# The expert loop of a decoder layer: four turns and seven steps behind it in place of three and twelve

## The chip, the cores and the metric

One core of one Trainium2 chip runs the whole layer. The time is that of one execution on the device, in microseconds (us), the median of several runs. A profile comes from one execution; its span is the time from the first to the last instruction that it recorded, so that the time of a run lies a little above it.

## What is computed

One decoder layer over 256 positions of 1024 features in float32: attention of two kinds and an output projection, then a mixture of experts. Each position takes 4 of 32 experts, and almost the whole traffic is the experts' weights, 8 MB for gate and up and 4 MB for down, per expert. Cut to the part that matters here:

```python
D_MODEL, SEQ, N_EXPERTS, TOP_K, D_FF = 1024, 256, 32, 4, 1024

def clamped_swiglu(h):
    x_glu = jnp.minimum(h[..., :D_FF], SWIGLU_LIMIT)
    x_lin = jnp.clip(h[..., D_FF:], -SWIGLU_LIMIT, SWIGLU_LIMIT)
    return x_glu * jax.nn.sigmoid(SWIGLU_ALPHA * x_glu) * (x_lin + 1.0)

def moe_ffn(h, w_router, b_router, w_gate_up, b_gate_up, w_down, b_down):
    ...
    logits = (xf @ w_router + b_router).astype(jnp.float32)
    top_vals, top_idx = lax.top_k(logits, TOP_K)
    gate = jax.nn.softmax(top_vals, axis=-1)
    ...
    def expert_block(args):
        xb, e = args
        hgu = xb @ w_gate_up[e] + b_gate_up[e]
        return clamped_swiglu(hgu) @ w_down[e] + b_down[e]
    ...
        x = x + moe_ffn(h2, w_router[l], b_router[l], w_gate_up[l], b_gate_up[l], w_down[l], b_down[l])
```

## The kernel before, in words

The front part (to about 165 us of the profile) is attention, the output projection and the router. Behind it stands a chain of steps, one for each expert and block of up to 64 positions; where no expert has more than 64 positions, as in the profiled data, there are 32 steps, 0 to 31.

**A step.** `step(n, it, g)` on TensorE does, in this order: `up` (the product with gate and up weights of expert k, in two pieces j = 0, 1, L1694), `gather` (the rows of a later expert, L1678), `down` (the down product of expert k-1, L1706), and `between` (turning the gathered rows, L1686, the slots, L1713, the up result, L1720, and adding the result of an earlier expert to the sum in four PSUM banks, L1728). ScalarE and VectorE have a `step` of their own each that copies and works on the results between these products. All of them keep step by semaphores.

**The weights.** They come in pieces of 4 MB, three for a step (up 0, up 1, down), into a ring of five pairs of slots (`pairs`, `NPAIR` = 5, the tiles `pair0` to `pair4`). The queue of SyncE (SP) issues the transfers, one whole piece each (`fetch`, L447), each as soon as TensorE has told by `used0` to `used4` that the pair is free (`free`). The last pieces of all are issued in parts (`rows_in_place`, L363), so that TensorE can start on the first rows while the others are on their way. `landed` and `arrived` are the waits of TensorE for a piece.

**The two places outside the ring.** Two buffers of 2 MB, `extra` and `extra2`, are loaded in the front part with the lower half (rows 4 to 7 of 8) of the down weights of two experts. They are read at the steps `KEPT` = (FIRST + 1, FIRST + 2), numbered from the end of the loop, and the ring brings only the upper half of those two. Which experts they are follows from `expert_behind`. Between these two steps TensorE also does what it owes the sum once: `keep_rows` adds the residual (L1647), `gated_bias` the gated biases of down (L1642), after a transpose of the gates (L1873).

**The loop.** Steps 0 to 4 are written out in front (`FIRST` = 5). Then every engine has a hardware loop (`Fori`) with a body of five steps (`NSTEP`), and behind it `LAST` steps written out. `GROUPS` holds the number of turns for one, two, three or four blocks of 64 positions per expert; the first entry, for one block, is ceil((32 - FIRST - LAST) / 5). The count is read from a register, and a second number, `shift`, skips the places that stay empty. The last two of the `LAST` steps have forms of their own, with the split transfers, and a last down product in two halves of the columns (L1946) with its own combine (L1959).

```python
        def expert_behind(n):
            return E - FIRST - LAST + n
...
            for c in range(first, last - 2):
                expert = expert_behind(expert_of(c))
                if c in (piece(n, 2) for n in KEPT):
                    free(c, groups)
                    rows_in_place(c % NPAIR, expert, 2, 0, 2, f"ring{c % NPAIR}")
                else:
                    fetch(c, groups, expert)
```

Of the kernel before, what the change touches and what calls it, by code (L numbers as in the profile page):

```python
# [43 lines left out]
PAIRS = ((4, 5), (0, 1), (6, 7), (2, 3), (8, 9))  # L44
NPAIR = len(PAIRS)
NSTEP = 5
FIRST, LAST = 5, 12
GROUPS = [-(-(E * (r + 1) - FIRST - LAST) // NSTEP) for r in range(ROUNDS)]
NPOS = NSTEP * GROUPS[-1] + FIRST + LAST + 1
SLOTW = 512 * DK  # L50
# [1946 lines left out]
```

How the kernel before makes its waits and increments, by code:

```python
        def front_arrived(eng, i):  # L279
            eng.wait_ge(s[f"stage{i % NSLOT}"], 16 * (i // NSLOT + 1))
# [10 lines left out]
        def landed(eng, c, g=None):  # L291
            n = 16 * (c // NPAIR + 1)
            eng.wait_ge(s[f"ring{c % NPAIR}"], n if g is None else g * (16 * USES) + n)
# [1 line left out]
        def arrived(eng, c, g=None):  # L295
            if c in PARTS:
                eng.wait_ge(s[PARTS[c][0]], 16 * PARTS[c][1])
            landed(eng, c, g)
# [1 line left out]
        def consumed(eng, c, g=None):  # L300
            n = c // NPAIR + 1
            eng.wait_ge(s[f"used{c % NPAIR}"], n if g is None else g * USES + n)
# [23 lines left out]
        def front_used(eng, i):  # L326
            kind, m = LOADS[i]
            if kind == "in":
                eng.wait_ge(s["proj_full"], NT * (m + 1))
            elif kind == "cmp":
                eng.wait_ge(s["h_full"], m + 1)
            else:
                eng.wait_ge(s["wo_full"], m + 3)
# [3 lines left out]
        @block.sync  # L337
# [27 lines left out]
            front_used(sp, 4)  # L365
            rows_in_place(0, 0, 0, 0, 2, "stage4")
            front_used(sp, 5)
            rows_in_place(0, 0, 0, 2, 4, "ring0")
            front_used(sp, 6)
            rows_in_place(1, 0, 1, 0, 2, "stage0")
            sp.wait_ge(s["u_full"], 1)
            rows_in_place(2, 1, 0, 0, 2, "stage6")
            front_used(sp, 7)
            rows_in_place(1, 0, 1, 2, 4, "ring1")
            sp.wait_ge(s["o_full"], 1)
            rows_in_place(2, 1, 0, 2, 4, "ring2")
            sp.wait_ge(s["oc_half"], 3)
            rows_in_place(4, 0, 2, 0, 2, "down0")
```

## Time and profile before

| | us |
|---|---|
| median of 3 runs | 1067.37 |
| lowest, highest | 1065.93, 1068.52 |
| span of the profiled execution | 1064.8 |
| TensorE busy in it | 1018.3 |

In the rows below, a line of the order of time reads: start (us), length (us), engine, line of the code, operation, result and operands by their names, number of instructions merged, and in brackets the idle time of the engine just before, with what ended it. A line of the windows reads: stretch, its length, TensorE's busy time with the number of instructions that started there, the granted clock as a share of full speed, the busy share of the DMA engines, and GB/s. Instructions are pipelined and lines are merged, so that the end of a line can reach a little into the next. `pair`, without its number, stands for each of the five pairs.

### The profile page before, as it was taken

The numbers are of one execution on the slowest core, as the hardware profiler recorded it, in microseconds if no ns is written. First come the engines' busy times: TensorE is split into PE (matmuls) and PEld (weight loads), VectorE is DVE, ScalarE is ACT, GpSimd is POOL, SyncE is SP. The second block draws the span as 40 slices with busy tenths as digits, with TensorE's granted clock in tenths as the row PEclk, the third lists the DMA queues.
The fourth block names the chain that finished last, engine by engine and source line by source line (L and its number), as shares of the span: only waits on it lengthen the run. The fifth ranks groups of instructions, "written<-read, shape, count | busy, mean of one in ns | idle before, by whom it ended". The sixth has DMA issues, their size and how long they took to land.

```text
span 1064.8 us, 12012 instructions
## 1 busy us (share of the span) xinstructions
PE 1018.3 (96%) x4969; PEld 410.9 (39%) x4969; DVE 293.2 (28%) x676; ACT 167.9 (16%) x325; POOL 15.9 (1%) x42
## 2 busy tenths in 40 slices
PE   8999999999999999999999999999999999899998
PEld 5555644333333333333333333333333333333334
DVE  1764614222222222211222122222112222222222
ACT  2434321111111111110110011111101111110011
POOL 4100000000000000000000000000000000000000
PEclk9999998999999999999999999999999999999999
DMA  9992668999999999999999999999999999999996
GB/s 295 363 409 84 251 263 320 426 424 435 431 430 430 432 429 431 431 433 432 432 431 430 432 432 433 433 432 429 429 429 429 431 433 431 431 432 431 420 425 264
DMA packets 36023, 426.45 MB, mean 400 GB/s; under 512 B 3782, under 2 KB 12062, under 8 KB 19728
## 3 DMA queue, kind: packets, MB, share of 16 engines
q1 hardware_dynamic: 34224, 424.78, 94.9%
q0 software_dynamic: 704, 1.04, 0.5%
q8 instruction: 29, 0.48, 0.2%
q10 hardware_dynamic: 1056, 0.07, 0.1%
q14 instruction: 10, 0.08, 0.0%
HBM read 424.83 MB, written 1.05 MB: 400 GB/s over the span
## 4 chain that ended last, share of the span: by engine, by line
PE 62%; DMA 34%; DVE 2%; SPq 1%; issue 1%; ACT 0%; ACTq 0%; DVEq 0%
DMA pair<-in_w_down 30%; PE bank L1694 24%; PE bank L1706 14%; PE bank L1316 5%; DMA pair<-in_w_gate_up 4%; PE bank L1728 4%; PE bank L1591 3%; PE bank L1678 2%; PE bank L1720 2%; PE bank L1686 1%; PE bank L1713 1%; PE bank L1388 1%; PE bank L1946 1%; SPq L363 1%; PE bank L1348 1%; DMA stage<-in_w_in 1%
## 5 line engine op out<-in xcount | busy, mean ns | idle before, releaser
L1694 PE MATMUL bank<-pair,xs 128*64 128x512 f32 x2048 | 450.0, 594 | 21.9 <-DMA pair<-in_w_gate_up 20.8
L1694 PEld LDWEIGHTS bank<-pair,xs 128*64 128x64 f32 x2048 | 143.1, 137 | 323.3 <-issue 285.9
L1706 PE MATMUL bank<-pair,sig 128*64 128x512 f32 x960 | 212.2, 593 | 13.4 <-DMA pair<-in_w_down 13.4
L1209 DVE COPY gu<-bank 128x512 f32<-128x512 f32 x32 | 36.5, 1140 | 416.2 <-PE bank L1694 416.2
L1706 PEld LDWEIGHTS bank<-pair,sig 128*64 128x64 f32 x960 | 72.3, 137 | 149.2 <-issue 143.4
L757 ACT COPY gu<-bank 128x512 f32<-128x512 f32 x32 | 36.4, 1138 | 457.1 <-PE bank L1694 457.1
L854 DVE TENSOR_TENSOR xs<-bank,gt 128x512 f32<-128x512 f32 x31 | 21.4, 691 | 220.6 <-PE bank L1686 220.6
L1316 PE MATMUL bank<-stage,xt 128*128 128x512 f32 x160 | 72.2, 598 | 0.0
L1728 PE MATMUL bank<-ys,pgt 64*128 64x512 f32 x248 | 61.6, 615 | 0.3 <-ACT ys L762 0.3
L1678 PE MATMUL bank<-xr,onehot 128*64 128x512 f32 x248 | 58.5, 592 | 0.0
L762 ACT COPY ys<-bank 128x512 f32<-128x512 f32 x31 | 18.1, 585 | 206.2 <-PE bank L1706 206.2
L1216 DVE TENSOR_TENSOR gu<-bank,bias_t 128x512 f32<-128x512 f32 x64 | 41.0, 682 | 2.7 <-PE bank L1720 2.7
L1316 PEld LDWEIGHTS bank<-stage,xt 128*128 128x128 f32 x160 | 29.2, 190 | 32.2 <-issue 31.6
L1720 PE MATMUL bank<-ident,gu 128*128 128x128 f32 x256 | 33.3, 273 | 0.0
L1678 PEld LDWEIGHTS bank<-xr,onehot 128*64 128x64 f32 x248 | 17.8, 137 | 35.4 <-issue 35.4
L774 ACT ACTIVATE sig<-gu 128x512 f32<-128x512 f32 x31 | 19.6, 631 | 71.0 <-DVE gu L1221 71.0
L1591 PE MATMUL bank<-stage,ot 128*128 128x512 f32 x64 | 28.8, 598 | 0.7 <-PE bank L1570 0.5
L1720 PEld LDWEIGHTS bank<-ident,gu 128*128 128x128 f32 x256 | 28.9, 141 | 1.6 <-ACT gu L757 0.8
L1728 PEld LDWEIGHTS bank<-ys,pgt 64*128 64x128 f32 x248 | 21.3, 186 | 20.1 <-issue 19.6
L1686 PEld LDWEIGHTS bank<-ident,xg 128*128 128x128 f32 x124 | 17.4, 210 | 24.3 <-issue 24.3
L1686 PE MATMUL bank<-ident,xg 128*128 128x128 f32 x124 | 23.1, 309 | 0.0
L1225 DVE SCALAR_TENSOR_TENSOR gu<-gu 128x512 f32<-128x512 f32 x32 | 22.2, 693 | 1.1
(310 smaller groups left out, 497.0 us busy)
## 6 DMA issues: line engine op xcount, KB each, us to landing
pair<-in_w_gate_up SPq DMA_DIRECT2D x51, 4096.0 KB, 39.8
pair<-in_w_down SPq DMA_DIRECT2D x24, 4096.0 KB, 38.0
pair<-in_w_gate_up SPq DMA_DIRECT2D x22, 2048.0 KB, 14.6
pair<-in_w_down SPq DMA_DIRECT2D x15, 1024.0 KB, 13.3
pair<-in_w_down SPq DMA_DIRECT2D x6, 2048.0 KB, 32.9
stage<-in_w_in SPq DMA_DIRECT2D x5, 2048.0 KB, 19.2
pair<-in_w_gate_up SPq DMA_DIRECT2D x8, 1024.0 KB, 4.8
stage<-in_w_out SPq DMA_DIRECT2D x2, 2048.0 KB, 15.2
```

Source lines behind the costliest of these rows:

```text
L757: nc.scalar.copy(gu[:, 0, :].rearrange("p (i q) -> p q i", i=FQ), up_banks[0][:].rearrange("p (q i) -> p q i", i=FQ)).then_inc(s["gu_hi"], 1)
L1209: V.tensor_copy(gu[:, 1, :].rearrange("p (i q) -> p q i", i=FQ), up_banks[1][:].rearrange("p (q i) -> p q i", i=FQ)).then_inc(s["gu_lo"], 1)
L1216: V.tensor_tensor(dst[:], up_banks[a][:].rearrange("p (c b n) -> p c b n", c=4, b=2), bias[:, a].to_broadcast([P, 4, 2, CAP]), ALU.add).th ...
L1225: V.scalar_tensor_tensor(out=lin[:], in0=lin[:], scalar=1.0, in1=glu[:], op0=ALU.add, op1=ALU.mult)\
L1316: last = mm(banks[PROJ_BANKS[n]][:, 0:width], xt[:, k, ti * P:(ti + 1) * P], front_slot(LOADS.index(("in", piece)))[:, k, 0:width], start= ...
L1591: last = mm(banks[2 * ti + m][:], ot[:, k, ti * P:(ti + 1) * P], front_slot(i)[:, k, :], start=k == 0, stop=k == DK - 1)
L1678: last = mm(x_bank[b * CAP:(b + 1) * CAP, :], onehot[:, ti, :], xr[:, ti, 512 * b:512 * (b + 1)], start=ti == 0, stop=ti == NT - 1)
L1686: last = tp(x_bank[:, c * P:(c + 1) * P], cols[:, c // UP_K, c % UP_K, :], ident[:])
L1694: last = mm(up_banks[a][b * CAP:(b + 1) * CAP, :].rearrange("p (q i) -> p q i", i=FQ), xs[:, k, :], cols[:, b], start=k == 0, stop=k == DK ...
L1706: last = mm(down_bank[b * CAP:(b + 1) * CAP, :], actf[:, kk % FQ, kk // FQ, :], row[:, 512 * b:512 * (b + 1)], start=kk == 0, stop=kk == D ...
L1720: last = tp(up_banks[a][:, c * P:(c + 1) * P], gu[:, a, c * P:(c + 1) * P], ident[:])
L1728: last = mm(banks[2 * ti + m][:], pgt[m * CAP:(m + 1) * CAP, ti * P:(ti + 1) * P], ys[m * CAP:(m + 1) * CAP, :], start=first, stop=True, s ...
```

## The change

One number changes:

```diff
 NPAIR = len(PAIRS)
 NSTEP = 5
-FIRST, LAST = 5, 12
+FIRST, LAST = 5, 7
 GROUPS = [-(-(E * (r + 1) - FIRST - LAST) // NSTEP) for r in range(ROUNDS)]
 NPOS = NSTEP * GROUPS[-1] + FIRST + LAST + 1
```

It sets these in turn:

| | before | after |
|---|---|---|
| `GROUPS` | 3, 10, 16, 23 | 4, 11, 17, 24 |
| `NPOS` | 133 | 133 |
| steps in the loop, for one block per expert | 5 to 19 | 5 to 24 |
| steps behind the loop | 20 to 31 | 25 to 31 |
| steps that read `extra`, `extra2` | 21, 22 | 26, 27 |
| experts whose lower down half they hold | 20, 21 | 25, 26 |
| residual and bias products, in front of the up product of step | 22 | 27 |

On TensorE, behind the loop, ahead of the last two steps: the names are those of the ring's pairs (numbers 89 to 93), of the gathered rows (`xs`), the one-hot matrix, the activations (`sig`) and the slots (`pgw`, `pgt`).

```order
 L1728 MATMUL bank<-ys,pgt 128x512 x4
 L1694 MATMUL bank<-pair_93,xs 64x512 x16
-L293 REGISTER_ALU
-L1694 MATMUL bank<-pair_89,xs 64x512 x16
-L1675 REGISTER_ALU
-L1678 MATMUL bank<-xr,onehot 64x512 x4
-L1706 MATMUL bank<-pair_90,sig 64x512 x16
-L1686 MATMUL bank<-ident,xg 128x128 x4
-L1713 MATMUL bank<-ident,pgw 128x128 x2
-L1720 MATMUL bank<-ident,gu 128x128 x8
-L1728 MATMUL bank<-ys,pgt 128x512 x4
```

This is the first of five steps in a row that are gone there; they are now done by the loop's fourth turn, ahead of the two steps with the kept halves, whose own instructions are the same as before.

On the queue of SP, behind the loop, ahead of the transfers that are issued in parts:

```order
 L447 DMA pair_93<-in_w_gate_up 128x8192
 L440 REGISTER_ALU
-L447 DMA pair_89<-in_w_gate_up 128x8192
-L447 DMA pair_90<-in_w_down 128x8192
-L447 DMA pair_91<-in_w_gate_up 128x8192
-L447 DMA pair_92<-in_w_gate_up 128x8192
-L447 DMA pair_93<-in_w_down 128x8192
-L440 REGISTER_ALU
```

Five of the fifteen whole pieces that no longer stand behind the loop; the two transfers of half a down piece stand ahead of these, and now have fifteen whole pieces fewer behind them.

## Rows read from the trace of the kernel before

**Rows 1.** The page: TensorE, and the rate of all transfers in 40 equal slices.
```profile
PE 1018.3 (96%) x4969; PEld 410.9 (39%) x4969; DVE 293.2 (28%) x676; ACT 167.9 (16%) x325; POOL 15.9 (1%) x42
...
GB/s 295 363 409 84 251 263 320 426 424 435 431 430 430 432 429 431 431 433 432 432 431 430 432 432 433 433 432 429 429 429 429 431 433 431 431 432 431 420 425 264
```

**Rows 2.** Windows, TensorE alone: stretch, length, busy (x), clock, DMA share, GB/s.
```profile
539.48:743.52 204.04, 187.62 (x883) 1.00 1.00 432
771.44:776.32 4.88, 4.88 (x21) 1.00 0.95 406
776.32:881.84 105.52, 105.50 (x508) 1.00 1.01 432
```

**Rows 3.** TensorE in order of time, the two waits of step 20.
```profile
722.78 7.09 PE L1694 MATMUL bank<-pair,xs 128*64 128x512 f32 x32 [1.33 <-DMA pair<-in_w_gate_up]
...
732.60 7.09 PE L1706 MATMUL bank<-pair,sig 128*64 128x512 f32 x32 [1.01 <-DMA pair<-in_w_down]
```

**Rows 4.** TensorE in order of time, steps 21 to 29.
```profile
751.92 7.09 PE L1694 MATMUL bank<-pair,xs 128*64 128x512 f32 x32 [1.32 <-DMA pair<-in_w_gate_up]
...
763.99 3.60 PE L1706 MATMUL bank<-extra,sig 128*64 128x512 f32 x16
...
776.32 13.95 PE L1694 MATMUL bank<-pair,xs 128*64 128x512 f32 x64
...
795.25 3.60 PE L1706 MATMUL bank<-extra,sig 128*64 128x512 f32 x16
...
898.13 7.09 PE L1706 MATMUL bank<-pair,sig 128*64 128x512 f32 x32 [0.61 <-DMA pair<-in_w_down]
...
947.82 7.09 PE L1694 MATMUL bank<-pair,xs 128*64 128x512 f32 x32 [1.60 <-DMA pair<-in_w_gate_up]
...
976.94 7.09 PE L1694 MATMUL bank<-pair,xs 128*64 128x512 f32 x32 [1.39 <-DMA pair<-in_w_gate_up]
...
986.75 7.09 PE L1706 MATMUL bank<-pair,sig 128*64 128x512 f32 x32 [1.00 <-DMA pair<-in_w_down]
```

**Rows 5.** TensorE in order of time, steps 30 and 31 and the end.
```profile
997.67 13.95 PE L1694 MATMUL bank<-pair,xs 128*64 128x512 f32 x64
1011.46 1.89 PE L1678 MATMUL bank<-xr,onehot 128*64 128x512 f32 x8
...
1024.05 10.52 PE L1694 MATMUL bank<-pair,xs 128*64 128x512 f32 x48
1035.61 3.65 PE L1694 MATMUL bank<-pair,xs 128*64 128x512 f32 x16 [1.03 <-DMA pair<-in_w_gate_up]
...
1050.65 5.40 PE L1946 MATMUL bank<-pair,xs 128*64 128x256 f32 x48 [0.15 <-DMA pair<-in_w_down]
```

**Rows 6.** DMA issues in 880:1065: count, KB each, median us from issue to landing.
```profile
pair<-in_w_gate_up SPq DMA_DIRECT2D x5, 4096.0 KB, 41.7
...
pair<-in_w_down SPq DMA_DIRECT2D x7, 1024.0 KB, 37.4
pair<-in_w_down SPq DMA_DIRECT2D x2, 2048.0 KB, 37.0
```

**Rows 7.** TensorE in order of time, the end of the loop's first turn.
```profile
423.95 1.99 PE L1728 MATMUL bank<-ys,pgt 64*128 64x512 f32 x8
425.87 13.95 PE L1694 MATMUL bank<-pair,xs 128*64 128x512 f32 x64
```

**Rows 8.** DMA queues in 440:735: packets, MB, share of 16 engines.
```profile
DMA packets 4369, 127.37 MB, mean 432 GB/s; under 512 B 482, under 2 KB 482, under 8 KB 482
...
q1 hardware_dynamic: 4369, 127.37, 100.3%
```

**Rows 9.** DMA queues in 735:890.
```profile
q8 instruction: 6, 0.10, 0.3%
```

**Rows 10.** DMA queues in 890:1060.
```profile
q8 instruction: 6, 0.10, 0.2%
```

## The prediction

> **What bounds the kernel now.** I read the page first: TensorE is busy for 96% of the span, and the transfers run at 429 to 435 GB/s in almost every slice behind the front part [rows 1]. Two resources are near their limit, so busy shares can't say which sets the time. The clock can't: the granted clock stands at 1.00 (the 2.4 GHz level) in every stretch used below [rows 2].
>
> Next come the windows by step, read on TensorE alone. Step k does the up product of expert k and the down product of expert k-1. Steps 22 to 25 (776.32 to 881.84) take 105.52 us, 26.38 each, with TensorE busy throughout [rows 2]. The seven steps of 539.48:743.52 take 204.04 us, 29.15 each, at the same transfer rate of 432 GB/s, and TensorE is busy for 187.62 of them [rows 2]. Those are the two paces: 26.38 us of products, 29.15 us to bring one expert's 12 MB. The difference is 2.77 us a step.
>
> Then the order of time on TensorE shows which pace holds where. From step 10 on it waits for a transfer twice a step, 1.33 and 1.01 us being typical [rows 3]. At the second up piece of step 21 it waits 1.32 us (751.92), and then not again until 898.13, in step 26 [rows 4]. Between them lie the two down products whose lower half (2 MB) has been in `extra` and `extra2` since the front part [rows 4]. The rotation fetches 4 MB less there. At 29.15 us for 12 MB that is 9.7 us of spare time. The four extra products for residual and bias in front of step 22 take 4.88 us of it [rows 2], and the rest goes at 2.77 us a step: the stretch holds 5.0 steps of work, and the stream and the products meet again in step 26. From there TensorE waits in steps 26 to 29, again once at 1035.61 and once at 1050.65 for the last rows [rows 4, 5]. So the end is set by the stream of weights, which never stops: each transfer is issued about 37 to 42 us ahead of its landing [rows 6], four pieces deep.
>
> **The change part by part.** (a) Work and bytes. Per expert nothing is added or removed: GROUPS goes from 3 to 4 turns of five steps, the steps behind the loop from 12 to 7, 5+15+12 = 5+20+7 = 32. The bytes are the same. Five unrolled steps less on every engine cost and save nothing by themselves, as the step in the loop has the same instructions.
>
> (b) One more turn of the loop. At the end of the first turn (425.87), where TensorE was never waiting for data, the last combine product (423.95, 1.99 us) is followed by the next step's first product with no idle time [rows 7]. The lower bound is 0. In the new kernel the extra turn ends at step 24, where TensorE waits 2.3 us in the step anyway [rows 3]: a stall of less than that disappears. I take 0. The Trainium skill ("Runtime: NRT & Kernel Launch", Instruction fetch mechanics) says that a taken branch to a page outside the two-page window must fetch it before execution goes on. By that rule every turn would stall; the trace disagrees at 425.87, with no idle time. The sum would be the same by either as long as the stall is under 2.3 us.
>
> (c) The kept halves move from steps 21 and 22 to 26 and 27, and the 4.88 us of products from in front of step 22 to in front of step 27. This is the term that counts. Before the kept halves nothing differs: TensorE starts the second up piece of step 21 at 751.92 in both. In the new kernel five more steps go at the pace of the stream: 5 x 29.15 = 145.7, so the second up piece of step 26 starts at 751.92 + 145.7 = 897.7. Then the old pattern follows, five steps later. From the second up piece of step 21 to the start of step 22 took 776.32 - 751.92 = 24.40 [rows 4], so step 27 starts at 922.1. Steps 27 to 30 find their data landed and take 4 x 26.38 = 105.5: step 31 starts at 1027.6. It started at 1024.05 before [rows 5]. That is 3.5 us later.
>
> Are the data really there? Old landings behind step 27 hold for the new kernel too, as the same bytes have been saved by then. In the old kernel the starts that waited mark them: second up pieces at 947.82, 976.94 (steps 28 and 29), last rows of step 31's up at 1035.61, first part of the last down at 1050.65 [rows 4, 5]. The new kernel wants those of 28 and 29 at 948.5 + 6.9 and 974.8 + 6.9, some 7.6 and 4.8 us after landing, and the rows of step 31 at 1027.6 + 10.3 = 1037.9, 2.3 us after landing. (10.3 is three quarters of an up product that doesn't wait, 1011.46 - 997.67 = 13.79 [rows 5].) So it doesn't wait there, and saves the old wait of 1.03 with its restart: from here it is 1037.9 - 1035.6 = 2.3 us late. The wait of 0.15 before the last down product goes as well [rows 5], which leaves 2.2. Behind it only TensorE, ScalarE and the writes of y follow one another, as before.
>
> (d) Issue times at the end. The rotation's last transfers are issued when TensorE frees a pair, 2 to 4 us later than before in steps 30 and 31. They were issued 37 us and more ahead of landing [rows 6], so this lies under pieces still queued: 0.
>
> (e) Instruction fetches. In 440:735, inside the second and third turn, all 4369 packets belong to the weights' queue; from 735 to 890 and from 890 to 1060 the instruction queue moves 6 packets each time, of 16 KB [rows 8 to 10]. At 431/16 GB/s each holds up one DMA engine for some 0.6 us (an estimate), and a piece has landed only when the slowest engine is done. Where there is no fetch, the rhythm is exact (722.78 to 751.92, 29.14 [rows 3, 4]). From 898.13 to 986.75 three steps take 88.62, 1.2 more than 3 x 29.15 [rows 4]. The new kernel has five steps less of straight code, all of them ahead of 890. This shortens the stream's end by up to 1.2 us, but the end isn't the stream's any more, so I take 0 and keep it for the range. Should the same 1.2 us fall ahead of 897.7, it adds to the sum.
>
> Sum: 3.5 - 1.2 (the wait of 1.03 and its restart) - 0.15 = **+2.2 us**. The profiled execution has a span of 1064.8 and would get 1067.0. The median of the runs is 1067.37, 2.6 above that span; the same step gives 1069.6.
>
> **The rivals.** (1) The end stays with the stream. The time is then unchanged, 1067.4. This decides if TensorE gets to the last up rows before they land: the margin worked out above is 2.3 us, so it needs landings that much later in the last part than this trace shows, or products that are 0.4 us a step shorter. Against it: 26.38 us recurs in all steps without a wait. For it: executions differ by 2.6 us between lowest and highest, and what comes late in the last 150 us is now covered. A milder form, in which the usual execution has a late landing or two more in the end part than the profiled one, gives 1067.5 to 1069. This is the rival on the other side: not slower.
>
> (2) The stream ends earlier by the fetches that are gone and TensorE isn't late, 1067.4 - 1.2 = 1066.2. It needs (1)'s condition as well. To be faster by more than 0.2% it would need twice the fetch saving.
>
> (3) The fetch delays fall ahead of 897.7. TensorE starts its last run of steps 1.2 us later and nothing gives that back: 1069.6 + 1.2 = 1070.8. For it: some straight code starts at step 25, around 885. Against it: one or two fetches only lie between there and 897.7.
>
> (4) The extra turn stalls TensorE, by the skill's rule above. It decides from 2.3 us on; a stall of 4 us would add 1.7 us, 1071.3. The row at 425.87 speaks against it.
>
> **How the numbers follow.** My forecast, TensorE late by 2.2 us, gets 0.62, rival (1) 0.21, (2) 0.03, (3) 0.12, (4) 0.02. A difference of 0.2%, 2.1 us, is about what a measurement of this kernel can tell from no change, and the forecast sits right at it. Its own range is 1068.6 to 1070.4, of which I give a little more than half to the upper side of 1069.5. That makes slower by more than that 0.35 + 0.12 + 0.02 = 0.49, within it 0.27 + 0.20 = 0.47, and faster 0.04 (from (2) and the edge of (1)). The range 1067.0 to 1071.2 leaves out most of (2) and (4).
>
> **What would show it.** In the profile of the changed kernel: starts after a wait go on at 29.15 us through steps 22 to 26; the last wait of a product for a weight transfer (but for the front) is at about 898; steps 27 to 30 take 26.38 each with no wait; the residual and bias products stand at about 917; step 31 starts 3.5 us later than before, and neither the last up rows nor the last down product waits. The instruction queue shows some five packets less. If waits for transfers are found after 930, the forecast is wrong and rival (1) is right. If the start near 897.7 is over 1 us late, it is (3); if there is idle time at the end of step 24 that no transfer ends, (4).

## The result, and the profile after

| | before | after |
|---|---|---|
| median, us | 1067.18 (21 runs) | 1068.58 (21 runs) |
| lowest, highest | 1065.93, 1068.52 | 1067.22, 1070.53 |
| ratio, 95% interval | | 1.0017 (1.0011 to 1.0023) |
| span of the profiled execution | 1064.8 | 1068.5 |

The ratio is 1.8 us of loss, with an interval from 1.2 to 2.5 us; the medians alone differ by 1.4 us. The interval doesn't reach zero, and lies on both sides of the 0.2% (2.1 us) that stood ahead as the bound. The changed kernel is slower by about as much as can be told apart. Two executions of the kernel before, in a later series, took 2132 and 3725 us and are left out of every difference below.

The page of the changed kernel answers to [rows 1]. The rate has the same plateau, and one line of the queues (name, packets, MB, share of 16 engines) has become smaller; it read 29 packets before.

```profile
PE 1020.9 (96%) x4969; PEld 412.4 (39%) x4969; DVE 292.9 (27%) x676; ACT 167.7 (16%) x325; POOL 15.8 (1%) x42
...
GB/s 292 363 406 86 236 276 306 426 427 435 431 430 431 429 431 431 432 432 432 432 432 432 433 432 432 432 432 432 432 432 432 432 432 430 430 429 430 422 424 217
...
q8 instruction: 24, 0.39, 0.2%
```

TensorE in order of time, the changed kernel, from step 21 on (lines as in [rows 3 to 5]):

```profile
753.14 7.09 PE L1694 MATMUL bank<-pair,xs 128*64 128x512 f32 x32 [1.32 <-DMA pair<-in_w_gate_up]
...
782.28 7.09 PE L1694 MATMUL bank<-pair,xs 128*64 128x512 f32 x32 [1.33 <-DMA pair<-in_w_gate_up]
...
899.31 7.09 PE L1694 MATMUL bank<-pair,xs 128*64 128x512 f32 x32 [1.80 <-DMA pair<-in_w_gate_up]
...
911.38 3.60 PE L1706 MATMUL bank<-extra,sig 128*64 128x512 f32 x16
...
923.70 13.96 PE L1694 MATMUL bank<-pair,xs 128*64 128x512 f32 x64
...
1029.23 13.96 PE L1694 MATMUL bank<-pair,xs 128*64 128x512 f32 x64
...
1054.35 5.40 PE L1946 MATMUL bank<-pair,xs 128*64 128x256 f32 x48
```

In [rows 4] the waits in brackets stop after 751.92 and are back at 898.13. Here they go on through step 26, and the one at 899.31 is the last of all: neither step 31 (1029.23) nor the last down product (1054.35) has one. TensorE has become the late partner, exactly in the last five steps.

The spans differ by 3.7 us, which is more than the runs do. 1.4 us of that arise in the first 17 us of the profiled executions, where the code of both kernels is the same. Before, then after, TensorE's first products of the front part:

```profile
6.15 1.09 PE L1296 MATMUL bank<-ident,xr 128*128 128x128 f32 x8
8.11 8.21 PE L1388 MATMUL bank<-stage,xt 128*128 128x296 f32 x32 [0.86 <-DMA stage<-in_w_in]
16.16 7.03 PE L1316 MATMUL bank<-stage,xt 128*128 128x512 f32 x16
```

```profile
6.52 1.97 PE L1296 MATMUL bank<-ident,xr 128*128 128x128 f32 x8
8.45 9.26 PE L1388 MATMUL bank<-stage,xt 128*128 128x296 f32 x32
17.54 7.03 PE L1316 MATMUL bank<-stage,xt 128*128 128x512 f32 x16
```

The eight transposes take 1.97 in place of 1.09 us, most of which goes into the wait of 0.86 us that is gone; the 32 products behind them take 9.26 in place of 8.21 us, and that is the larger part of the 1.4. Among the experiments below loop3_kept26 has the short form and loop3_kept25, whose code is the same there, the long one; so it belongs to the execution, not to the change. From a profile of each alone one would have read 3.7 us. What the change does is read from a stretch with both ends behind the front part: from the second up piece of step 21 to the start of the last down product it is 1050.65 - 751.92 = 298.73 before and 1054.35 - 753.14 = 301.21 after, 2.5 us more. This stretch is called the end stretch below.

### The profile page after: what moved, and what is told of

It is laid out like the page before. It is cut to its first block, busy times and chain, and to the rows that moved or that the text cites. A ratio compares the mean times of both kernels' runs of the same rounds, so it can differ in the third digit from the quotient of the medians.

```text
span 1068.5 us, 12055 instructions
## 1 busy us (share of the span) xinstructions
PE 1020.9 (96%) x4969; PEld 412.4 (39%) x4969; DVE 292.9 (27%) x676; ACT 167.7 (16%) x325; POOL 15.8 (1%) x42
## 4 chain that ended last, share of the span: by engine, by line
PE 66%; DMA 30%; DVE 2%; issue 1%; ACT 0%; SPq 0%; DVEq 0%
DMA pair<-in_w_down 26%; PE bank L1694 26%; PE bank L1706 15%; PE bank L1316 5%; PE bank L1728 4%; DMA pair<-in_w_gate_up 4%; PE bank L1591 3%; PE bank L1678 3%; PE bank L1720 2%; PE bank L1686 1%; PE bank L1713 1%; PE bank L1388 1%; PE bank L1946 1%; PE bank L1348 1%; PE bank L1375 1%; PE bank L1358 1%
```

## The experiments

Two theories stood against each other. **K**: the loss comes from where the kept halves are read; the end is set by the later of stream and TensorE. **L**: it comes from the loop, one turn more or less straight code. All times below are differences from the kernel before by the ratio of the runs, with the 95% interval. "loop3" and "loop4" stand for three turns (twelve steps behind) and four (seven behind), and the number behind "kept" for the step that reads `extra`.

### The place of the kept halves alone

loop3_kept26, the kernel before with one line changed:

```diff
-KEPT = (FIRST + 1, FIRST + 2)
+KEPT = (FIRST + 6, FIRST + 7)
```

> The kernel before (three turns, twelve steps behind the loop) with the kept halves and the residual and bias products moved to steps 26 and 27, nothing else. Theory K (the end is set by the later of stream and TensorE, and what counts is how few steps follow the kept halves): the same as the change, 1.8 to 2.3 us slower than before; no wait of TensorE for a weight transfer after about 898, step 31 starts 3.5 us later than before relative to the landings. Rival L (the fourth turn, or the shorter straight code, is what costs): no difference from before, under 0.5 us.

Measured: +2.7 us (+1.5 to +3.9). The loop is the old one and the loss is there in full: L falls. TensorE in order of time shows the second up piece of step 21, the last wait, and the start of step 31 and of the last down product:

```profile
752.27 7.09 PE L1694 MATMUL bank<-pair,xs 128*64 128x512 f32 x32 [1.33 <-DMA pair<-in_w_gate_up]
...
897.97 7.09 PE L1694 MATMUL bank<-pair,xs 128*64 128x512 f32 x32 [1.33 <-DMA pair<-in_w_gate_up]
...
1027.88 13.95 PE L1694 MATMUL bank<-pair,xs 128*64 128x512 f32 x64
...
1053.00 5.40 PE L1946 MATMUL bank<-pair,xs 128*64 128x256 f32 x48
```

This execution has the short front part, as the one before, and can be held against the prediction's numbers as they stand: 897.7, 1027.6, and a last down product 2.2 us behind 1050.65, which is 1052.9.

loop3_kept25, one step earlier, `KEPT = (FIRST + 5, FIRST + 6)`:

> The kernel before (three turns) with the kept halves at steps 25 and 26 and the residual and bias products in front of step 26. K: TensorE starts its run of steps without a wait one step earlier than in loop3_kept26, 2.8 us nearer to the landings, and meets them again just at the last up rows (0.6 us too early): time as before, within 0.7 us. If the cost grows evenly with the distance of the move, four fifths of the change's: 1.4 us or more.

Measured: -0.5 us (-1.4 to +0.4). One step less, and the whole loss is gone. TensorE at step 21, its last wait before its run of steps, and what it meets at the end:

```profile
753.25 7.09 PE L1694 MATMUL bank<-pair,xs 128*64 128x512 f32 x32 [1.32 <-DMA pair<-in_w_gate_up]
...
869.82 7.09 PE L1694 MATMUL bank<-pair,xs 128*64 128x512 f32 x32 [1.34 <-DMA pair<-in_w_gate_up]
...
1036.96 3.65 PE L1694 MATMUL bank<-pair,xs 128*64 128x512 f32 x16 [0.32 <-DMA pair<-in_w_gate_up]
...
1052.00 5.40 PE L1946 MATMUL bank<-pair,xs 128*64 128x256 f32 x48 [0.15 <-DMA pair<-in_w_down]
```

The bracket of 0.32 us at the last up rows is the point where stream and TensorE meet; 0.6 had been worked out.

loop4_kept27, the changed kernel one step later, `KEPT = (FIRST + 2, FIRST + 3)`:

> The changed kernel with the kept halves read one step later still, at steps 27 and 28 (residual and bias products in front of step 28). K: one more step goes at the stream's 29.15 us in place of 26.38, so 2.8 us more than the change: 4.6 to 5.0 us slower than before. L: as the change, 1.8 us.

Measured: +5.2 us (+3.7 to +6.8), where L had 1.8. The last wait is now one step later, and no other follows:

```profile
753.82 7.09 PE L1694 MATMUL bank<-pair,xs 128*64 128x512 f32 x32 [1.32 <-DMA pair<-in_w_gate_up]
...
928.66 7.09 PE L1694 MATMUL bank<-pair,xs 128*64 128x512 f32 x32 [1.32 <-DMA pair<-in_w_gate_up]
...
1057.31 5.40 PE L1946 MATMUL bank<-pair,xs 128*64 128x256 f32 x48
```

loop4_again is the change itself, beside others of the second series:

> The change itself, beside the others of this call: 1.3 to 2.3 us slower than before, 2 us or more slower than loop4_rows_early_again.

Measured: +2.1 us (+1.2 to +3.1). Its second up pieces of steps 21 and 26, the last wait for a transfer, and its last down product:

```profile
752.71 7.09 PE L1694 MATMUL bank<-pair,xs 128*64 128x512 f32 x32 [1.34 <-DMA pair<-in_w_gate_up]
...
898.44 7.09 PE L1694 MATMUL bank<-pair,xs 128*64 128x512 f32 x32 [1.34 <-DMA pair<-in_w_gate_up]
...
1053.48 5.40 PE L1946 MATMUL bank<-pair,xs 128*64 128x256 f32 x48
```

Together, with the end stretch of each profiled execution:

| kept halves read at | 21, 22 | 25, 26 | 26, 27 (three turns) | 26, 27 (four turns) | 27, 28 |
|---|---|---|---|---|---|
| us against before, by the runs | 0 | -0.5 | +2.7 | +1.8 and +2.1 | +5.2 |
| end stretch, us against 298.73 | 0 | 0.0 | +2.0 | +2.5 and +2.0 | +4.8 |
| worked out from the rows | 0 | 0 | +2.2 | +2.2 | +5.0 |

The times at 21 and at 25 are alike, and behind them each step adds about one pace difference, 2.8 us (some 2 us for the first, part of which the stream still covers): the form of a maximum of two times, not of a cost that grows with the distance of the move.

### TensorE's work in the end part

loop4_rows_early takes the four residual products (x8 in the trace) out of the part where TensorE is the late one:

```diff
             between(2)
...
+            keep_rows()
             for n in range(3, FIRST):
                 step(n, n, None)
...
                     pe.wait_ge(s["late"], 16 * N_LATE)
-                    keep_rows()
                     pe.wait_ge(s["gtt"], 1)
```

> The changed kernel with its four residual products (3.6 us of the 4.88) done behind step 2, where pieces have landed ahead of TensorE, in place of in front of step 27. K: TensorE reaches the last up rows 3.6 us earlier, 1.3 us before they land, waits once more at the end, and the time goes back to that of before, within 0.5 us. L: stays 1.8 us slower. Third possibility: the products delay the stream where they stand now (pairs are freed 3.6 us later), and the time is 1.8 us or more slower.

It ran three times, in three series, as two more questions came up:

> The same kernel as loop4_rows_early, beside the others of this call on one chip: its first time was 0.7 us under before with an interval from -1.7 to +0.2. If that was real, 0.5 to 1 us faster than before again; if not, 0 +- 0.5 us.

> The partner of loop1_kept26_rows_early on the same chip: within 0.7 us of before, as in its two earlier measurements.

Measured: -0.7 (-1.7 to +0.2), -0.2 (-1.2 to +0.7) and -0.2 us (-1.3 to +0.9). The loss of the change is gone, and a gain over the kernel before isn't shown: the -0.7 of the first time didn't come again. 3.6 us of TensorE's work were taken away from there, but step 27 starts only 2.7 us sooner: from the second up piece of step 26 to it are 918.62 - 896.97 = 21.65 us, against 24.39 in the change, as the bias products now wait for ScalarE. The end stretch is 298.85 us (1050.09 - 751.24) in the first of the three, 1.9 to 2.4 us under that of the change; the rest runs into the stream, and the last down product waits again:

```profile
751.24 7.09 PE L1694 MATMUL bank<-pair,xs 128*64 128x512 f32 x32 [1.33 <-DMA pair<-in_w_gate_up]
...
896.97 7.09 PE L1694 MATMUL bank<-pair,xs 128*64 128x512 f32 x32 [1.33 <-DMA pair<-in_w_gate_up]
...
917.55 1.14 PE L1642 MATMUL bank<-bdn,gtt 32*128 32x512 f32 x8 [0.62 <-ACT gtt L796]
918.62 13.95 PE L1694 MATMUL bank<-pair,xs 128*64 128x512 f32 x64
...
1050.09 5.40 PE L1946 MATMUL bank<-pair,xs 128*64 128x256 f32 x48 [0.39 <-DMA pair<-in_w_down]
```

The second execution has this wait too (0.36 us), the third has none. That the products delay the stream where they stand now, the third possibility, is excluded: the kernel isn't slower.

loop3_rows_early is the same edit on the kernel before:

> The kernel before with the same residual products done behind step 2. K: TensorE's next wait for weights after step 21 comes a step or so later than 898, the end is still set by the stream: no difference, within 0.5 us. If instead TensorE's total work sets the end (the step of my prediction that reads the end as the stream's is wrong): up to 3.6 us faster.

Measured: +1.0 us (0.0 to +2.0). There is no gain of 3.6 us, so that TensorE's total work doesn't set the end of the kernel before. Two things of what I had written missed. The next wait comes earlier, not later:

```profile
753.61 7.09 PE L1694 MATMUL bank<-pair,xs 128*64 128x512 f32 x32 [1.33 <-DMA pair<-in_w_gate_up]
...
870.89 7.09 PE L1706 MATMUL bank<-pair,sig 128*64 128x512 f32 x32 [0.80 <-DMA pair<-in_w_down]
```

870.89 and not 898.13: a TensorE with less to do eats up its spare data sooner. And the time is above the 0.5 us that I allowed by the middle of its interval, which reaches from 0.0 to +2.0. Its cause stays open. The question of the next part came from the distance to loop4_rows_early, which has more turns and less straight code; but that can't explain the distance to the kernel before, which has the same loop and the same 29 packets on the instruction queue.

### The loop and the straight code

loop3_kept26_rows_early differs from loop4_rows_early by the loop alone:

> Three turns of the loop, kept halves at 26 and 27, residual products behind step 2: it differs from loop4_rows_early by the loop alone (five steps of straight code more, one turn less). K without an effect of the loop: the same time as loop4_rows_early, within 0.5 us. Rival F (each fetch of straight code delays the stream's slowest DMA engine, and here the stream sets the end): 0.5 to 1.5 us slower than loop4_rows_early.

Measured: +0.7 us (-0.2 to +1.6), against -0.2 for its partner in the same series. 0.9 us in the direction of F, with intervals that overlap: not settled. So the dose was raised. loop1_kept26_rows_early:

```diff
-FIRST, LAST = 5, 7
+FIRST, LAST = 5, 22
...
-KEPT = (FIRST + 1, FIRST + 2)
+KEPT = (FIRST + 16, FIRST + 17)
```

> One turn of the loop and 22 steps behind it, kept halves at steps 26 and 27, residual products behind step 2: loop4_rows_early with 15 steps more of straight code. The stream sets its end. Rival F (the fetches of straight code delay the stream): three times the difference of loop3_kept26_rows_early and loop4_rows_early, 1.5 to 3 us slower than loop4_rows_early_third. Without such an effect: the same, within 0.5 us.

Measured: +3.0 us (+1.9 to +4.1), against -0.2 for its partner: 3.2 us for fifteen steps, 0.2 us for each step of straight code. The intervals don't touch, and the difference lies just above the 1.5 to 3 us that F expected: straight code costs time here. The page of this kernel has 39 packets on the instruction queue, the partner's 24. In the stretch 440:735 it moves ten of them, where the partner, in its loop, moves none:

```profile
DMA packets 4368, 127.10 MB, mean 431 GB/s; under 512 B 482, under 2 KB 482, under 8 KB 482
...
q8 instruction: 10, 0.16, 0.2%
```

TensorE in order of time, the same kernel, shows where it arises. The waits of the second up piece, 1.32 us where nothing disturbs, are longer in some steps:

```profile
490.09 7.09 PE L1694 MATMUL bank<-pair,xs 128*64 128x512 f32 x32 [0.98 <-DMA pair<-in_w_gate_up]
...
606.88 7.09 PE L1694 MATMUL bank<-pair,xs 128*64 128x512 f32 x32 [1.33 <-DMA pair<-in_w_gate_up]
...
636.45 7.09 PE L1694 MATMUL bank<-pair,xs 128*64 128x512 f32 x32 [1.76 <-DMA pair<-in_w_gate_up]
...
724.73 8.78 PE L1694 MATMUL bank<-pair,xs 128*64 128x512 f32 x32 [2.01 <-DMA pair<-in_w_gate_up]
...
754.10 7.09 PE L1694 MATMUL bank<-pair,xs 128*64 128x512 f32 x32 [1.08 <-DMA pair<-in_w_gate_up]
...
871.10 7.09 PE L1694 MATMUL bank<-pair,xs 128*64 128x512 f32 x32 [1.78 <-DMA pair<-in_w_gate_up]
...
900.41 7.09 PE L1694 MATMUL bank<-pair,xs 128*64 128x512 f32 x32 [1.50 <-DMA pair<-in_w_gate_up]
```

The partner in its loop, the same two starts:

```profile
490.26 7.09 PE L1694 MATMUL bank<-pair,xs 128*64 128x512 f32 x32 [0.56 <-DMA pair<-in_w_gate_up]
...
752.52 7.09 PE L1694 MATMUL bank<-pair,xs 128*64 128x512 f32 x32 [1.33 <-DMA pair<-in_w_gate_up]
```

Over these nine steps the partner takes 262.3 us and this kernel 264.0, 1.7 us more, in the profiled execution, which is the fastest of its runs (1068.66 us, median 1070.39). From 606.88 to 636.45 it is 29.57 us for a step in place of 29.14; other steps have a fetch and stay at 29.14. The runs show the sum. That it comes about through the instruction fetches is argued from the count of packets, not shown: no run has the straight code without them, and why one fetch would count and another not stays open.

## Why the prediction was right

The time was forecast as 1069.6 with a range from 1067.0 to 1071.2, and measured as 1068.58. The range holds the 1067.4 of rival (1) too, and 1068.58 lies just under the forecast's own 1068.6 to 1070.4 and inside the 1067.5 to 1069 of that rival's milder form. So the number alone doesn't decide. The traces do: rival (1) needs waits for transfers at the end, and neither the changed kernel nor loop4_again has one behind step 26. Of the 1.0 us by which the forecast was high, 0.2 is its starting point (1067.37 from three runs, 1067.18 from 21); the rest is 2.2 worked out against 1.4 between the medians, or 1.8 by the ratio of the runs. Whether the usual execution of the kernel before has a later landing at the end than the profiled one, as the milder form says, can't be told from one profile; it may be part of this rest.

The mechanism was the one put down, and the terms can be checked one by one against the rows above. To keep the execution's front part out, each stands as a stretch.

- **(a), (b)**: the extra turn ends at step 24. TensorE in order of time there, in the changed kernel, shows the last combine product of the turn and the first product behind the loop with no idle time between them; rival (4), a stall at the branch, didn't occur.

```profile
859.36 1.99 PE L1728 MATMUL bank<-ys,pgt 64*128 64x512 f32 x8
861.28 7.09 PE L1694 MATMUL bank<-pair,xs 128*64 128x512 f32 x32
```

- **(c), the pace of the stream for five more steps**: 145.7 worked out, 899.31 - 753.14 = 146.2 measured. The 0.5 us more are in the last of these steps, whose wait is 1.80 in place of 1.33. It is what rival (3) describes, at less than half its size, and it didn't come again: 898.44 - 752.71 = 145.7 in loop4_again, and 897.97 - 752.27 = 145.7 in loop3_kept26.
- **the old pattern behind it**: 24.40 worked out, 923.70 - 899.31 = 24.39 measured.
- **four steps at 26.38**: 105.5 worked out, 105.53 measured. This is the stretch on which rival (1) hung, and nowhere in it is there a wait.
- **step 31**: 26.60 us before, less 1.3 to 1.4 by the waits that go; 25.12 measured, 1.5 less.

The sum over the end stretch is +2.5 in this pair of profiles, and +2.0 with loop4_again, against +2.2 worked out. By the ratio of the runs it is +1.8, and +2.1 in the second series; 2.2 lies in both intervals.

**The reason given in step (e) was only half of one.** I took nothing for the fetches that are gone, since "the end isn't the stream's any more". But TensorE's last run starts at the landing near 897.7, so that every delay of the stream ahead of it counts in full for the end. The zero was right for another reason: the sum goes from 751.92 to 897.7 at 29.15 us a step, the pace of the loop, in which there are no fetches, and so there was no delay in it to take off. The straight code between 735 and 890 is what the change removes; six packets of the instruction queue before [rows 9], one after:

```profile
q8 instruction: 1, 0.02, 0.0%
```

In the profiles no gain from this can be seen: loop3_kept26 has these fetches and takes 145.7 us to step 26 all the same, and its end stretch, 300.7, is as long as that of loop4_again, 300.8. By the runs loop3_kept26 (+2.7) is above the change (+1.8, +2.1), which would agree with some 0.2 us for each of five steps, but the intervals overlap. (The window of [rows 8] also goes 20 us past the loop, whose third turn ends at 714.37; there is no fetch in these either.)

**The spare time was added up the wrong way.** The prediction lets the 4.88 us of products for residual and bias take part of the 9.7 us of spare time. They add to it: while TensorE does them, the stream runs on, and TensorE falls further behind the landings. 9.7 - 4.9 would last 1.7 steps at 2.77 us each; 9.7 + 4.9 = 14.6 last 5.3, and it is five steps that the rows show. loop3_rows_early bears this out. There step 22 starts 2.7 us sooner (775.27 - 753.61 = 21.66 us behind the second up piece of step 21, not 24.40), which leaves 11.9 us, or 4.3 steps, and the waits are back one step earlier, in step 25. The expectation of that run had the sign wrong for the same reason. The forecast didn't suffer: its sum takes the 24.40 us from the rows and never uses this count.

The Trainium skill ("Runtime: NRT & Kernel Launch", Instruction fetch mechanics) calls the cost of crossing a 16 KB block of instructions mostly hidden. For TensorE's own dispatch nothing here speaks against it. In this kernel, whose weights keep the DMA engines busy at 431 to 432 GB/s, the measurement differs: fifteen more steps of straight code, with fifteen more packets on the instruction queue, cost 3.2 us.

## What to carry to other kernels

Where transfers and an engine run at nearly the same pace, the time is the later of two chains, and data kept aside in advance is of use only if enough steps follow in which the engine can catch up with it: here about five (9.7 us of spare time and 4.9 of extra work, 14.6 together, used up at 2.8 us a step; the end comes some 2 us too soon when the reserve is read at step 26). Work that only the engine does, put just behind the reserve, makes this stretch longer, not shorter. Put such a reserve well ahead of the end; at 21 or at 25 the time was the same within the noise. One-off work for the busy engine goes where the engine waits anyway if the engine is the late one at the end; where the stream is, moving it gained nothing (+1.0 us, 0.0 to +2.0). Compare two profiles between marks behind the part that differs by execution, not by their spans.

## What the runs showed of the hardware that I had not expected

- In the second and later turns of a loop of five steps, some 635 products and as many weight loads on TensorE, the instruction queue moved nothing at all ([rows 8]), and the branch left no gap ([rows 7]). Unrolled code moved one packet of 16 KB a step (10 in 295 us), and cost 0.2 us a step in the runs.
- The first 17 us come in more than one form, up to 1.4 us apart, in executions of the same code. Of the twelve profiles, six take 8.2 us for the 32 products at 8 us (L1388) and six 9.1 to 9.5; the eight transposes ahead of them take from 1.09 to 1.97 us. The windows give a granted clock of 1.00 for 5:10 in both kernels, so the records don't name the cause; it stays open.
- A longer wait of TensorE was twice followed by a lower clock, and once not. In loop1_kept26_rows_early, after the wait of 2.01 us at 724.73, the windows (length, busy, clock, DMA share, GB/s) show less than the 2.4 GHz level for a few us, and the 32 products take 8.78 us in place of 7.09:

```profile
700.00:724.70 24.70, 21.71 (x104) 1.00 1.01 432
724.70:729.70 5.00, 4.97 (x16) 0.66 1.00 433
729.70:754.10 24.40, 23.32 (x112) 1.00 1.00 429
```

The mean of 0.66 is a stretch at 1.2 GHz within the 5 us. It cost nothing there: the next wait, at 754.10, is 1.08 us in place of 1.32. In loop3_rows_early a wait of 2.23 us was followed by 8.74 us for the same 32 products; in the kernel before one of 2.26 us wasn't:

```profile
949.48 8.74 PE L1694 MATMUL bank<-pair,xs 128*64 128x512 f32 x32 [2.23 <-DMA pair<-in_w_gate_up]
```

```profile
918.39 7.09 PE L1694 MATMUL bank<-pair,xs 128*64 128x512 f32 x32 [2.26 <-DMA pair<-in_w_gate_up]
```

So the length of the wait alone doesn't decide it.
